# Depthwise convolution of a Conformer block: four channel tiles on TensorE from stacked shifted copies, four on VectorE

## The chip, the cores and the metric

The kernel runs on one core of a Trainium2 chip. The metric is device time in microseconds of one execution. Engines are named as in the profile: PE is TensorE's matmul side and PEld its weight load, DVE is VectorE, ACT is ScalarE, POOL is GpSimd, SP is SyncE, which here only issues DMA transfers.

## What is computed

A two-layer trunk on 512 tokens of width 1024: layer 0 is a causal Conformer convolution module and a top-2 mixture of 16 experts; layer 1 is sliding-window attention and the same kind of mixture. All is float32. The change concerns only the depthwise filter of this function (`CONV_WIDTH` is 31, `D_MODEL` 1024):

```python
def conformer_conv(x, w1, b1, dw, dwb, g, bn, w2, b2):
    h = x @ w1 + b1
    a, gate = jnp.split(h, 2, axis=-1)
    h = a * jax.nn.sigmoid(gate)
    h = lax.conv_general_dilated(
        h, dw[:, None, :].astype(h.dtype), window_strides=(1,),
        padding=[(CONV_WIDTH - 1, 0)], dimension_numbers=('NWC', 'WIO', 'NWC'),
        feature_group_count=D_MODEL) + dwb
    h = jax.nn.silu(layer_norm(h, g, bn))
    return h @ w2 + b2
```

Each channel is filtered by itself with 31 taps along the tokens.

## The kernel before

The kernel is written engine by engine. Each engine runs its own program in the order written, and the order between engines is held by semaphores: `wait_ge` and `then_inc`. There is no scheduler.

Channels lie on partitions in eight tiles of 128; tokens lie along the free dimension. `arena` is one buffer that holds `xT` (x transposed), `hpad` (the gated activations with 30 zero columns ahead), `cv` (the filtered result) and small pieces such as `odd` and `sgm`. `wring` is a ring of six slots of 2 MB for weights.

The first projection (L514) writes, for channel tile c, 8 matmuls of `a` and 8 of `gate` into two PSUM banks and signals `s_g1`. ScalarE takes the sigmoid of the gate (L1308, `s_sgm`). VectorE's `glu(c)` (L883) adds the bias, multiplies and writes `hpad` (`s_glu`). From tile 4 on, the projection waits for the `glu` of the tile four before it, to have its banks back.

Channel tiles 0 to 5 are filtered on VectorE: `taps(c)` has two opening instructions (L892, L894), 29 taps (L898) that alternate between two accumulators, and a closing sum (L901). Tiles 6 and 7 are filtered on TensorE: for each of 31 taps GpSimd has built a diagonal 128x128 matrix of that tap's weights (`diag(c)`, L1563, one instruction of 3968 columns for a tile), and 31 matmuls of 512 columns (L526) accumulate in one PSUM bank. ScalarE evicts the bank with the bias (L1316). Since the TensorE tiles are wanted early, VectorE's order is `glu` 0, `taps` 0, ..., `taps` 3, then `glu` 4, `glu` 6, `taps` 4, `glu` 5, `glu` 7, `taps` 5.

After that, `stage_a` to `stage_d` on TensorE transpose the result, normalise it, apply the second projection (L552), and route. The experts follow (L616 for gate and up, L626 for down). Each of their products has 64 rows of tokens; the stationary operand has 64 columns, and two products alternate between the lower and the upper 64 PSUM partitions:

```python
for j in range(4):
    for h in range(2):
        mm = pe.matmul(ps[h * CAP:(h + 1) * CAP, bank, :],
                       act[:, j % 2, (j // 2) * CAP:(j // 2 + 1) * CAP],
                       w[:, j, h * 512:(h + 1) * 512], start=(j == 0), stop=(j == 3))
```

In the trace one float32 matmul stands as two passes (two MATMUL records and two LDWEIGHTS records), so 62 matmuls of L526 are 124.

SyncE's queue after the convolution's weights: gate of expert 0 into slot 0 as soon as two channel tiles are projected, up after four, down after `s_pec` 1 and gate of expert 1 after `s_pec` 2 (`s_pec` counts tiles filtered on TensorE), then loads that wait for later stages. GpSimd scales x and adds the second projection's bias (L1557, L1558) before it builds the diagonals.

## Time and profile before

| | us |
|---|---|
| three runs | 1270.77, 1277.02, 1279.67 |
| median | 1277.02 |
| the profiled execution, its time | 1279.67 |
| the profiled execution, its span from first to last instruction | 1279.7 |
| PE busy | 1033.9 (81%) |
| DVE busy | 485.0 (38%) |
| POOL busy | 199.6 (16%) |
| ACT busy | 168.2 (13%) |

The busy shares are means over the whole program. The convolution stage lies in its first sixth; its limits are read from the chain of waits and from the timelines of that stretch, not from these shares. The span is the profiled execution's whole time, so nothing lies around it.

### The profile page before, as it was taken

What the parts mean: (1) busy time and instruction counts of PE and PEld (TensorE: products, weight loads), DVE (VectorE), ACT (ScalarE), POOL (GpSimd) and SP (SyncE); (2) the same over time, 40 slices, a digit from 0 to 9 for tenths busy, and PEclk for the clock granted to TensorE, in tenths of its full rate; (3) what the DMA queues carried; (4) which work ended last, traced back from release to release, by engine and by line L of the source; (5) the groups of instructions that cost most, each with busy time, mean ns of one, the idle gap of its engine ahead of it and who ended that gap; (6) DMA issues with size and microseconds to landing.
All of it is one profiled execution on the core that took longest, in us unless ns stands there. A gap on an engine that the chain in (4) does not pass through costs nothing.

```text
span 1279.7 us, 15066 instructions
## 1 busy us (share of the span) xinstructions
PE 1033.9 (81%) x5458; PEld 552.4 (43%) x5459; DVE 485.0 (38%) x1003; ACT 168.2 (13%) x375; POOL 199.6 (16%) x257
## 2 busy tenths in 40 slices
PE   5999597993799889999488899968369777999950
PEld 3444244542455445455134444534245444555520
DVE  1799991446111011101285456564510000110117
ACT  0000002212000000000103332432200000000010
POOL 2243601112200100100241002021210010000013
PEclk8999798986799999999788799878679898999985
DMA  9930011206399999988790001300738999897863
GB/s 296 401 116 0 0 66 66 82 34 223 116 345 380 356 401 338 381 290 361 253 323 39 1 1 66 148 1 34 246 104 314 382 391 390 296 378 294 359 217 112
DMA packets 59726, 275.04 MB, mean 215 GB/s; under 512 B 5469, under 2 KB 13833, under 8 KB 51352
## 3 DMA queue, kind: packets, MB, share of 16 engines
q1 hardware_dynamic: 40368, 226.50, 47.1%
q10 hardware_dynamic: 12952, 28.03, 5.9%
q0 software_dynamic: 6352, 19.77, 5.1%
q8 instruction: 36, 0.59, 0.2%
q14 instruction: 18, 0.15, 0.0%
HBM read 252.48 MB, written 21.80 MB: 214 GB/s over the span
## 4 chain that ended last, share of the span: by engine, by line
PE 60%; DMA 14%; DVE 12%; issue 9%; POOL 2%; ACT 2%; SPq 0%; DVEq 0%; ACTq 0%; POOLq 0%
PE ps L616 20%; PE ps L626 10%; PE ps L755 5%; DMA wring<-in_moe_w_gate_dram 5%; DMA wring<-in_moe_w_up_dram 5%; PE ps L552 5%; PE ps L526 4%; PE ps L774 4%; PE ps L609 3%; DVE arena L898 2%; DMA wring<-in_conv_w_dram 1%; PE ps L514 1%; POOL vareps L1590 1%; DVE bns L917 1%; PE ps L800 1%
## 5 line engine op out<-in xcount | busy, mean ns | idle before, releaser
L616 PE MATMUL ps<-wring,arena 128*64 128x256 f32 x2624 | 314.3, 396 | 40.1 <-DMA wring<-in_moe_w_gate_dram 18.3
L616 PEld LDWEIGHTS ps<-wring,arena 128*64 128x64 f32 x2624 | 195.2, 143 | 154.3 <-issue 54.6
L626 PE MATMUL ps<-wring,arena 128*64 128x512 f32 x688 | 157.0, 598 | 6.8 <-DVE arena L1108 5.7
L898 DVE SCALAR_TENSOR_TENSOR arena<-arena,dwT 128x512 f32<-128x512 f32 (+1 forms) x174 | 125.4, 799 | 0.0
L514 PE MATMUL ps<-arena,wring 128*128 128x512 f32 x256 | 113.1, 604 | 9.3 <-DMA wring<-in_conv_w_dram 9.3
L1095 DVE COPY arena<-ps 128x256 f32<-128x256 f32 x32 | 13.6, 425 | 239.6 <-PE ps L670 239.6
L755 PE MATMUL ps<-wring,arena 128*128 128x512 f32 x192 | 91.0, 631 | 6.3 <-DMA wring<-in_attn_wq_dram 2.9
L626 PEld LDWEIGHTS ps<-wring,arena 128*64 128x64 f32 x688 | 46.1, 136 | 85.3 <-issue 74.9
L514 PEld LDWEIGHTS ps<-arena,wring 128*128 128x128 f32 x256 | 49.4, 194 | 71.6 <-issue 71.6
L526 PE MATMUL ps<-arena,wring 128*128 128x512 f32 x124 | 55.9, 614 | 12.9 <-DVE arena L883 12.9
L1590 POOL TENSOR_SCALAR vareps<-mv 128x1 f32<-128x1 f32 x20 | 21.6, 1082 | 274.0 <-DVE mv L919 273.9
L1619 POOL COPY idx<-tokT 64x1 uint32 (+1 forms) x32 | 5.8, 181 | 374.2 <-PE ps L609 368.6
L1089 DVE TENSOR_TENSOR arena<-arena,ps 128x256 f32<-128x256 f32 x32 | 13.5, 422 | 132.1 <-PE ps L616 132.1
L774 PE MATMUL ps<-wring,arena 128*128 128x512 f32 x128 | 62.1, 641 | 0.0
L552 PE MATMUL ps<-wring,arena 128*128 128x512 f32 x128 | 60.5, 630 | 1.9 <-ACT arena L1328 1.3
L755 PEld LDWEIGHTS ps<-wring,arena 128*128 128x128 f32 x192 | 38.1, 204 | 52.9 <-issue 51.8
L609 PE MATMUL ps<-ident,arena 64*128 64x64 f32 x344 | 47.1, 279 | 10.5 <-DMA arena<-x_dram,idx 10.5
L609 PEld LDWEIGHTS ps<-ident,arena 64*128 64x128 f32 x344 | 41.2, 199 | 31.5 <-issue 31.5
L1369 ACT ACTIVATE arena<-ps 128x512 f32<-128x512 f32 x32 | 19.1, 597 | 268.3 <-PE ps L626 268.3
L1609 POOL DMA_INDIRECT arena<-x_dram,idx x43 | 39.9, 928 | 32.4 <-POOL idx L1619 24.1
L526 PEld LDWEIGHTS ps<-arena,wring 128*128 128x128 f32 x124 | 24.3, 197 | 44.5 <-issue 30.8
L774 PEld LDWEIGHTS ps<-wring,arena 128*128 128x128 f32 x128 | 25.8, 208 | 31.6 <-issue 31.6
(209 smaller groups left out, 933.0 us busy)
## 6 DMA issues: line engine op xcount, KB each, us to landing
wring<-in_moe_w_up_dram SPq DMA_DIRECT2D x32, 2048.0 KB, 20.7
wring<-in_moe_w_down_dram SPq DMA_DIRECT2D x32, 2048.0 KB, 13.4
wring<-in_moe_w_gate_dram SPq DMA_DIRECT2D x30, 2048.0 KB
y_dram<-arena ACTq DMA_DIRECT2D x86, 128.0 KB, 8.1
wring<-in_conv_w_dram SPq DMA_DIRECT2D x8, 1024.0 KB, 11.7
wring<-in_conv_w_dram SPq DMA_DIRECT2D x2, 2048.0 KB, 17.8
y_dram<-arena ACTq DMA_DIRECT2D x1, 4096.0 KB, 27.7
x_dram<-x_sb ACTq DMA_DIRECT2D x8, 512.0 KB, 3.1
```

Source lines behind the costliest of these rows:

```text
L514: last = pe.matmul(ps[:, 2 * (c % 4) + h, :], w[:, k, h, (c % 2) * P:(c % 2) * P + P], xT[:, k, :], start=(k == 0), stop=(k == KD - 1))
L526: last = pe.matmul(ps[:, 2 * (c % 4) - 4, :], diag(c)[:, k, :], hpad[:, c, k:k + S], start=(k == 0), stop=(k == CW - 1))
L552: last = pe.matmul(ps[:, 4 + h, :], hc[t % 2][:, c, :], slot(4 + c // 4, 4)[:, c % 4, h * 512:(h + 1) * 512], start=(c == 0), stop=(c == K ...
L609: last = pe.transpose(ps[:, 0, j * CAP:(j + 1) * CAP], src[0:CAP, j::KD], ident[0:CAP, 0:CAP])
L616: mm = pe.matmul(ps[h * CAP:(h + 1) * CAP, bank, 0:256], act[:, k, :], w[:, k, h * 256:(h + 1) * 256], start=(k == 0), stop=(k == KD - 1))
L626: mm = pe.matmul(ps[h * CAP:(h + 1) * CAP, bank, :], act[:, j % 2, (j // 2) * CAP:(j // 2 + 1) * CAP], w[:, j, h * 512:(h + 1) * 512], sta ...
L755: last = pe.matmul(ps[:, bank, :], xTt[:, k, :], slot(at, KD)[:, k, :], start=(k == 0), stop=(k == KD - 1))
L774: last = pe.matmul(ps[:, bank, :], oT[t % 2][:, k, :], slot(3 + h, KD)[:, k, :], start=(k == 0), stop=(k == KD - 1))
L898: dve.scalar_tensor_tensor(out=acc, in0=hpad[:, one, k:k + S], scalar=dwT[:, one, k:k + 1], in1=acc, op0=ALU.mult, op1=ALU.add).then_inc(s ...
L1369: act.activation(ysb[b], ps[:, 4, :], ACT.Copy).then_inc(s_yc, 1)
L1590: own(pool.tensor_scalar(vareps[:, n:n + 1], mv[:, n, 1:2], EPS, None, ALU.add))
L1609: pool.indirect_dma_start(out=where[0:CAP, :], out_offset=None, in_=x_dram[:, :], in_offset=bass.IndirectOffsetOnAxis(ap=idx[:, idx_col:id ...
```

## The change

DVE_TILES goes from 6 to 4: VectorE filters channel tiles 0 to 3, TensorE 4 to 7. TensorE's way of filtering is another. The tile's 128 channels are four groups of 32. For group q, SyncE copies the group's 32 rows of `hpad` four times into a ring slot, each copy on 32 partitions of its own and shifted by s = 0..3 columns (`replicate`, 16 small transfers a tile). One matmul with 128 rows and 32 output columns then applies four taps at once to 32 channels; eight rounds with the moving operand advanced by four columns make 32 taps, the last being zero. The four groups of a round write the four 32-partition parts of one PSUM bank. The stationary operands of all rounds and groups (`wdw`, 128 partitions x 4096) are made by one GpSimd multiply of `wrep` (the weights, loaded by eight small transfers into `dw_a` and transposed on TensorE) and `fold` (which partition belongs to which of 32 channels, a VectorE reduction of the identity). `wdw` takes ring slot 0, the copies of tiles 4, 5, 6, 7 take slots 1, 2, 3, 1. VectorE's loop becomes straight code with each `glu` set between taps of an earlier tile. The first expert's loads wait for all four TensorE tiles.

```diff
-DVE_TILES = 6
+DVE_TILES = 4
+SHIFTS = 4
+GRP = P // SHIFTS
+ROUNDS = 8
+REPW = S + SHIFTS * (ROUNDS - 1)
...
+        dw_a = view(14080, SHIFTS, GRP)
+        wrep = view(14208, P)
+        fold = view(14336, GRP)
...
+        wdw = wring[:, 0, :].rearrange("p (r g n) -> p r g n", r=ROUNDS, g=SHIFTS * (KD - DVE_TILES))
+
+        def shifted(c):
+
+            slot_of = (1, 2, 3, 1)[c - DVE_TILES]
+            return wring[:, slot_of, 0:SHIFTS * REPW].rearrange("p (g n) -> p g n", g=SHIFTS)
...
-            sp.wait_ge(s_g1, 2)
+            def replicate(c):
+
+                sp.wait_ge(s_glu, c + 1)
+                for s in range(SHIFTS):
+                    for q in range(SHIFTS):
+                        sp.dma_start(shifted(c)[s * GRP:(s + 1) * GRP, q, :],
+                                     hpad[q * GRP:(q + 1) * GRP, c, s:s + REPW]).then_inc(s_rep[c - DVE_TILES], 16)
+
+            replicate(4)
+            replicate(5)
+            sp.wait_ge(s_g1, KD)
+            replicate(6)
+            sp.wait_ge(s_pec, 1)
+            replicate(7)
+            sp.wait_ge(s_pec, KD - DVE_TILES)
             gate(0, 0, 0)
-            sp.wait_ge(s_g1, 4)
             up(0, 0, 0)
-            sp.wait_ge(s_pec, 1)
             down(0, 0, 0)
-            sp.wait_ge(s_pec, 2)
             gate(0, 1, 1)
...
-                for c in range(KD):
+                for c in range(DVE_TILES):
                     pe.transpose(ps[:, 4, 32 * c:32 * c + CW], dw_r[:, c * P:(c + 1) * P], ident[0:CW, 0:CW])
+                pe.wait_ge(s_dwload, 16 * ROUNDS)
+                pe.transpose(ps[:, 5, P:2 * P], dw_a.rearrange("p s c -> p (s c)"), ident[:, :])
...
+            pe.wait_ge(s_wdw, 1)
             for c in range(DVE_TILES, KD):
-                pe.wait_ge(s_glu, glu_count(c))
-                pe.wait_ge(s_diag, c - DVE_TILES + 1)
-                for k in range(CW):
-                    last = pe.matmul(ps[:, 2 * (c % 4) - 4, :], diag(c)[:, k, :], hpad[:, c, k:k + S],
-                                     start=(k == 0), stop=(k == CW - 1))
+                pe.wait_ge(s_glu, c + 1)
+                pe.wait_ge(s_rep[c - DVE_TILES], 16 * SHIFTS * SHIFTS)
+                for r in range(ROUNDS):
+                    for q in range(SHIFTS):
+                        last = pe.matmul(ps[q * GRP:(q + 1) * GRP, 2 * (c % 4), :],
+                                         wdw[:, r, SHIFTS * (c - DVE_TILES) + q, :],
+                                         shifted(c)[:, q, SHIFTS * r:SHIFTS * r + S],
+                                         start=(r == 0), stop=(r == ROUNDS - 1))
                 last.then_inc(s_pec, 1)
...
+            dve.tensor_copy(wrep, ps[:, 5, P:2 * P])
+            dve.wait_ge(s_pool0, 2)
+            dve.tensor_reduce(fold, ident[:, :].rearrange("p (s j) -> p j s", s=SHIFTS), AX.X, ALU.add)
...
-            with dve.Fori(0, 2) as i:
-                for b in range(2):
-                    glu(2 * i + b, b)
-                    taps(2 * i + b, 2 * i + (b + 1))
-            glu(4, 0)
-            glu(6, 0)
-            taps(4, glu_count(4))
-            glu(5, 1)
-            glu(7, 1)
-            taps(5, glu_count(5))
+            glu(0)
+            taps(0, {18: 1})
+            taps(1, {4: 2, 22: 3})
+            taps(2, {7: 4, 26: 5})
+            taps(3, {10: 6, 28: 7})
...
+            act.wait_ge(s_dwzero, 1)
+            groups = SHIFTS * (KD - DVE_TILES)
+            for r in range(ROUNDS):
+                n = min(SHIFTS, CW - SHIFTS * r)
+                act.dma_start(dw_a[groups * r:groups * (r + 1), 0:n, :],
+                              conv_dw[0, SHIFTS * r:SHIFTS * r + n, P * DVE_TILES:].rearrange("s (g c) -> g s c", c=GRP)
+                              ).then_inc(s_dwload, 16)
...
             pool.wait_ge(s_prC, 1)
-            for c in range(DVE_TILES, KD):
-                pool.wait_ge(s_g1, c if c < KD - 1 else KD)
-                pool.affine_select(out=diag(c), in_=dwT[:, c, 0:CW].unsqueeze(2).to_broadcast([P, CW, P]),
-                                   compare_op=ALU.is_equal, fill=0.0, base=0, pattern=[[0, CW], [-1, P]],
-                                   channel_multiplier=1).then_inc(s_diag, 1)
+            pool.wait_ge(s_g1, 2)
+            pool.tensor_tensor(wdw.rearrange("p r g n -> p (r g) n"), wrep.unsqueeze(2).to_broadcast([P, P, GRP]),
+                               fold.unsqueeze(1).to_broadcast([P, P, GRP]), ALU.mult).then_inc(s_wdw, 1)
```

In `taps(1, {4: 2, 22: 3})` the table says that `glu(2)` stands before tap 4 and `glu(3)` before tap 22 of channel tile 1.

TensorE, from the last tile of the projection to the first transpose of `stage_a`, before (L514 the projection, L526 the diagonal matmuls, L483 the transposes):

```order
L514 MATMUL ps<-arena,wring 128x512 [waits s_glu,s_w1_3]
L514 MATMUL ps<-arena,wring 128x512 x15
L526 MATMUL ps<-arena,wring 128x512 [waits s_diag,s_glu]
L526 MATMUL ps<-arena,wring 128x512 x30
L526 MATMUL ps<-arena,wring 128x512 [waits s_diag,s_glu]
L526 MATMUL ps<-arena,wring 128x512 x30
L483 MATMUL ps<-ident,arena 128x128 [waits s_tap,s_pecv]
```

and with the change (L534 the projection, L548 the new matmuls, L501 the transposes):

```order
L534 MATMUL ps<-arena,wring 128x512 [waits s_glu,s_w1_3]
L534 MATMUL ps<-arena,wring 128x512 x15
L548 MATMUL ps<-wring 32x512 [waits s_rep0,s_glu,s_wdw]
L548 MATMUL ps<-wring 32x512 x31
L548 MATMUL ps<-wring 32x512 [waits s_rep1,s_glu]
L548 MATMUL ps<-wring 32x512 x31
L548 MATMUL ps<-wring 32x512 [waits s_rep2,s_glu]
L548 MATMUL ps<-wring 32x512 x31
L548 MATMUL ps<-wring 32x512 [waits s_rep3,s_glu]
L548 MATMUL ps<-wring 32x512 x31
L501 MATMUL ps<-ident,arena 128x128 [waits s_tap,s_pecv]
```

Two runs of 31 matmuls with 128 output columns have become four runs of 32 with 32 output columns, and each run waits for its own copies (`s_rep0` to `s_rep3`).

SyncE, from the second projection's weights on, before:

```order
L403 DMA wring<-in_conv_w_dram 128x4x1024 x2
L406 DMA wring<-in_moe_w_gate_dram 128x4096 [waits s_g1]
L409 DMA wring<-in_moe_w_up_dram 128x4096 [waits s_g1]
L412 DMA wring<-in_moe_w_down_dram 128x4x1024 [waits s_pec]
L406 DMA wring<-in_moe_w_gate_dram 128x4096 [waits s_pec]
```

and with the change (`wring<-arena` are the copies):

```order
L447 DMA wring<-arena 32x540 [waits s_glu]
L447 DMA wring<-arena 32x540 x15
L447 DMA wring<-arena 32x540 [waits s_glu]
L447 DMA wring<-arena 32x540 x15
L447 DMA wring<-arena 32x540 [waits s_glu,s_g1]
L447 DMA wring<-arena 32x540 x15
L447 DMA wring<-arena 32x540 [waits s_glu,s_pec]
L447 DMA wring<-arena 32x540 x15
L413 DMA wring<-in_moe_w_gate_dram 128x4096 [waits s_pec]
L416 DMA wring<-in_moe_w_up_dram 128x4096
L419 DMA wring<-in_moe_w_down_dram 128x4x1024
L413 DMA wring<-in_moe_w_gate_dram 128x4096
```

Four runs of 16 transfers stand ahead of the first expert's loads, and these now wait for the last of the filtered tiles only.

VectorE, its last two channel tiles before (L883 `glu`, L892 and L894 openers, L898 taps, L901 sum):

```order
L883 SCALAR_TENSOR_TENSOR arena<-ps,prmT,arena 128x512 x2
L892 TENSOR_SCALAR arena<-arena,dwT,prmT 128x512
L894 TENSOR_SCALAR arena<-arena,dwT 128x512
L898 SCALAR_TENSOR_TENSOR arena<-arena,dwT 128x512 x29
L901 TENSOR_TENSOR arena<-arena 128x512
L883 SCALAR_TENSOR_TENSOR arena<-ps,prmT,arena 128x512 x2
L892 TENSOR_SCALAR arena<-arena,dwT,prmT 128x512
L894 TENSOR_SCALAR arena<-arena,dwT 128x512
L898 SCALAR_TENSOR_TENSOR arena<-arena,dwT 128x512 x29
L901 TENSOR_TENSOR arena<-arena 128x512
```

and the last channel tile with the change (L909 `glu`, L917 and L921 openers, L927 taps, L930 sum), after the sum of the tile before:

```order
L930 TENSOR_TENSOR arena<-arena 128x512
L917 TENSOR_SCALAR arena<-arena,dwT,prmT 128x512
L921 TENSOR_SCALAR arena<-arena,dwT 128x512
L927 SCALAR_TENSOR_TENSOR arena<-arena,dwT 128x512 x8
L909 SCALAR_TENSOR_TENSOR arena<-ps,prmT,arena 128x512
L927 SCALAR_TENSOR_TENSOR arena<-arena,dwT 128x512 x18
L909 SCALAR_TENSOR_TENSOR arena<-ps,prmT,arena 128x512
L927 SCALAR_TENSOR_TENSOR arena<-arena,dwT 128x512 x3
L930 TENSOR_TENSOR arena<-arena 128x512
```

The two `glu` of the TensorE tiles stand between taps now, `glu(7)` three taps before the end.

## Rows read from the trace of the kernel before

**Rows 1.** Chain of waits: shares by engine, then pieces (start us, us, what)
```profile
PE 60%; DMA 14%; DVE 12%; issue 9%; POOL 2%; ACT 2%; SPq 0%; DVEq 0%; ACTq 0%; POOLq 0%
...
328.00 9.64 PE ps L616 x64
```

**Rows 2.** Timeline of TensorE (start us, us, engine line operation count [idle before <-releaser])
```profile
37.99 96.46 PE L514 MATMUL ps<-arena,wring 128*128 128x512 f32 x224
...
147.37 55.89 PE L526 MATMUL ps<-arena,wring 128*128 128x512 f32 x124 [12.91 <-DVE arena L883]
...
204.03 1.09 PE L483 MATMUL ps<-ident,arena 128*128 128x128 f32 x8 [0.78 <-ACT arena L1316]
```

**Rows 3.** Timeline of VectorE: the weight copy, then pieces of channel tiles 0 to 5
```profile
38.29 0.41 DVE L873 COPY dwT<-ps 128x248 f32<-128x248 f32 x1
...
40.97 0.55 DVE L892 TENSOR_SCALAR arena<-arena,dwT,prmT  x1 [0.41 <-DVE arena L883]
...
93.41 0.69 DVE L901 TENSOR_TENSOR arena<-arena 128x512 f32 x1
...
115.58 4.09 DVE L901 TENSOR_TENSOR arena<-arena 128x512 f32 x1
...
146.56 0.75 DVE L883 SCALAR_TENSOR_TENSOR arena<-ps,prmT,arena 128x512 f32<-128x512 f32 x1 [0.89 <-ACT arena L1308]
...
148.11 20.28 DVE L898 SCALAR_TENSOR_TENSOR arena<-arena,dwT 128x512 f32<-128x512 f32 x29
...
171.33 0.54 DVE L892 TENSOR_SCALAR arena<-arena,dwT,prmT 128x512 f32<-128x512 f32 x1
...
172.18 19.30 DVE L898 SCALAR_TENSOR_TENSOR arena<-arena,dwT 128x512 f32<-128x512 f32 x29
...
191.51 0.69 DVE L901 TENSOR_TENSOR arena<-arena 128x512 f32<-128x512 f32 x1
```

**Rows 4.** GpSimd beside VectorE's taps: timeline; taps' durations, two windows; GpSimd groups
```profile
76.66 2.92 POOL L1558 TENSOR_TENSOR x_sb<-x_sb,rows 128x1024 f32<-128x1024 f32 x1
...
107.07 12.06 POOL L1563 TENSOR_SCALAR_AFFINE_SELECT wring<-dwT 128x3968 f32<-128x3968 f32 x1 [27.49 <-PE ps L514]
...
L898 DVE SCALAR_TENSOR_TENSOR arena<-arena,dwT x23: 737/740/2831, 53.8 to 81.4; - x12, 128x512 f32<-128x512 f32 x11
...
L898 DVE SCALAR_TENSOR_TENSOR arena<-arena,dwT x13: 743/744/746, 106.9 to 114.8; - x7, 128x512 f32<-128x512 f32 x6
...
L1684 POOL TENSOR_TENSOR x_sb<-x_sb,rows 128x1024 f32<-128x1024 f32 x4 | 9.6, 2394 | 0.3
```

**Rows 5.** L626's passes in narrow windows (busy, x open passes); chain in the experts
```profile
348.09:348.20 0.11, 0.10 (x2) 1.00 1.10 298
...
348.57:348.62 0.05, 0.05 (x4) 1.00 0.82 164
...
343.54 3.60 PE ps L616 x32
...
348.17 3.58 PE ps L626 x16
```

**Rows 6.** Timelines of DMA issues: ScalarE's queue, SyncE's queue
```profile
1.45 0.57 ACTq L1277 DMA_DIRECT2D prm<-in_conv_dwb_dram  x1
...
2.06 0.28 ACTq L1278 DMA_DIRECT2D prm<-in_conv_ln_g_dram  x1
...
0.85 1.83 SPq L397 DMA_DIRECT2D x_sb<-in_x_dram  x4
...
52.02 0.34 SPq L406 DMA_DIRECT2D wring<-in_moe_w_gate_dram  x1
```

**Rows 7.** DMA issues in 0 to 340 us (KB each, median us to landing)
```profile
x_sb<-in_x_dram SPq DMA_DIRECT2D x4, 512.0 KB, 5.2
...
tok_r<-tok_dram POOLq DMA_DIRECT2D x1, 32.0 KB, 2.5
```

**Rows 8.** Busy time by stretch: the experts of layer 0
```profile
328.00:613.00 285.00, 263.98 (x1935) 148.46 (x1936) 32.30 (x63) 20.41 (x42) 21.89 (x39) 0.97 0.90 338
```

More of the change, by code:

```diff
@@ L168, in view @@
             return v
-        PADW = S + CW - 1
+        PADW = REPW + SHIFTS
         xT = view(0, KD, S)
@@ L235, in trunk @@
         s_tap = sem("s_tap")
-        s_diag = sem("s_diag")
+        s_dwzero = sem("s_dwzero")
+        s_dwload = sem("s_dwload")
+        s_wdw = sem("s_wdw")
+        s_rep = [sem(f"s_rep{i}") for i in range(KD - DVE_TILES)]
         s_pec = sem("s_pec")
@@ L367, in taken @@
             eng.wait_ge(bank_read[bank - 5], n)
-        glu_order = [0, 1, 2, 3, 4, 6, 5, 7]
-        def glu_count(c):
-            return glu_order.index(c) + 1
-        def diag(c):
-            return wring[:, 2 + c - DVE_TILES, 0:CW * P].rearrange("p (k n) -> p k n", k=CW)
+        wdw = wring[:, 0, :].rearrange("p (r g n) -> p r g n", r=ROUNDS, g=SHIFTS * (KD - DVE_TILES))
+        def shifted(c):
+            slot_of = (1, 2, 3, 1)[c - DVE_TILES]
+            return wring[:, slot_of, 0:SHIFTS * REPW].rearrange("p (g n) -> p g n", g=SHIFTS)
         def slot(i, *dims):
@@ L861, in own @@
                 dve.wait_ge(s_dc, done[0])
+            dve.memset(dw_a.rearrange("p s c -> p (s c)"), 0.0).then_inc(s_dwzero, 1)
             for t in range(T):
@@ L874, in _, with glu @@
                             ).then_inc(s_prC, 1)
-            dve.wait_ge(s_pool0, 2)
             dve.wait_ge(s_prC, 1)
-            def glu(c, parity):
-                one = bass.ds(c, 1)
-                bank = 2 * c if not isinstance(c, int) else 2 * (c % 4)
+            def glu(c):
                 dve.wait_ge(s_g1, c + 1)
                 dve.wait_ge(s_sgm, c + 1)
-                dve.scalar_tensor_tensor(out=hpad[:, one, CW - 1:PADW], in0=ps[:, bass.ds(bank, 1), :],
-                                         scalar=prmT[:, bass.ds(c + PB1, 1)], in1=sgm[parity],
+                dve.scalar_tensor_tensor(out=hpad[:, c, CW - 1:CW - 1 + S], in0=ps[:, 2 * (c % 4), :],
+                                         scalar=prmT[:, PB1 + c:PB1 + c + 1], in1=sgm[c % 2],
@@ L885, in glu @@
                                          op0=ALU.add, op1=ALU.mult).then_inc(s_glu, 1)
             def taps(c, glus):
-                one = bass.ds(c, 1)
-                even = cv[:, one, :]
-                dve.wait_ge(s_glu, glus)
-                dve.tensor_scalar(even, hpad[:, one, 0:S], dwT[:, one, 0:1],
-                                  prmT[:, bass.ds(c + PDWB, 1)], ALU.mult, ALU.add).then_inc(s_tap, 1)
-                dve.tensor_scalar(odd, hpad[:, one, 1:1 + S], dwT[:, one, 1:2], None, ALU.mult).then_inc(s_tap, 1)
+                even = cv[:, c, :]
@@ L895, in taps @@
+                dve.wait_ge(s_glu, c + 1)
+                dve.tensor_scalar(even, hpad[:, c, 0:S], dwT[:, c, 0:1], prmT[:, PDWB + c:PDWB + c + 1],
+                                  ALU.mult, ALU.add).then_inc(s_tap, 1)
+                if c:
+                    dve.wait_ge(s_tap, c * (CW + 1))
+                dve.tensor_scalar(odd, hpad[:, c, 1:1 + S], dwT[:, c, 1:2], None, ALU.mult).then_inc(s_tap, 1)
                 for k in range(2, CW):
+                    if k in glus:
+                        glu(glus[k])
@@ L896, in taps @@
                     acc = (even, odd)[k % 2]
                     dve.wait_ge(s_tap, c * (CW + 1) + (k - 1))
-                    dve.scalar_tensor_tensor(out=acc, in0=hpad[:, one, k:k + S], scalar=dwT[:, one, k:k + 1],
+                    dve.scalar_tensor_tensor(out=acc, in0=hpad[:, c, k:k + S], scalar=dwT[:, c, k:k + 1],
                                              in1=acc, op0=ALU.mult, op1=ALU.add).then_inc(s_tap, 1)
@@ L1306, in _ @@
                 if c >= 2:
-                    act.wait_ge(s_glu, glu_count(c - 2))
+                    act.wait_ge(s_glu, c - 1)
                 act.activation(sgm[c % 2], ps[:, 1 + 2 * (c % 4), :], ACT.Sigmoid,
@@ L1524, in _ @@
             pool.memset(cv[:, KD - 1, :], 0.0)
+            pool.memset(hpad[:, :, CW - 1 + S:PADW], 0.0)
             pool.memset(hpad[:, :, 0:CW - 1], 0.0).then_inc(s_pool0, 1)
```

5 lines of the change are left out of this document (3 added, 2 removed).

## The prediction

> **What bounds the kernel now.** I read the chain of waits first. TensorE is 60% of it, and its list in order of time holds one block that belongs to this change: the 124 passes of L526 from 147.37 to 203.26, the depthwise filters of channel tiles 6 and 7 [rows 1, 2]. The reader is to see what stands on both sides of that block. Ahead of it TensorE idles 12.91 us, because it has finished the first projection at 134.45 but VectorE reaches `glu(6)` only at 146.56 [rows 3]; behind it ScalarE evicts and `stage_a` begins at 204.03 [rows 2]. So the end of the stage is VectorE's first four tiles, then 56 us of TensorE. VectorE's own last tile ends at 192.20 [rows 3]: 11 us of cover, no more. Everything after 203.3 (the rest of layer 0, attention, experts) is fed by that one point. Nothing that the change touches comes later, except loads of the first expert's weights. So the gain or loss is the shift of the point 203.26.
>
> **Work that goes.** TensorE loses 62 full matmuls, 55.89 us. VectorE loses two channel tiles. A tile in the clear costs it 20.87 us, 171.33 to 192.20: two openers, 29 taps at 0.665 (19.30/29), one sum [rows 3]. The pause around each `glu`, 0.4 us before and after, goes too, since a `glu` now sits between taps of an earlier tile and costs 0.67. GpSimd loses two diagonal builds, one of them 12.06 us; it did not slow the taps (13 of them at 0.743 to 0.746 us in its window), but the closing sum of a tile waited it out: 4.09 instead of 0.69 us [rows 3, 4].
>
> **TensorE's new work.** Each of four tiles takes 8 rounds of 4 matmuls, with 32 output columns each; a matmul stays two passes in the trace. A 512-column pass alone costs 96.46/224 = 0.4306 us [rows 2]. What four passes on four column groups cost together is the question on which all hangs. The nearest rows are the experts' products, where two groups of 64 columns alternate. In L626 two passes stand in the record at once from the start: 2 in the window 348.09 to 348.20, 4 from 348.57 as the next pair enters before the first drains; 16 passes take 3.58 us, 0.224 each, and 32 passes of half the width take 3.60 us [rows 5]. So two groups run wholly beside each other. Moreover the first pair starts together: if a pass waited behind all passes ahead of it, the second pass of the first matmul would have to go before the other group's first, and the first pass would stand alone. I read that as a queue for each group, in which case four groups overlap as well: 0.4306/4 = 0.1077 us a pass, 64 passes = 6.9 us a tile, 27.6 us for four. The bounds: as two groups do, 0.2153 a pass and 13.8 us a tile; with no overlap, 27.6 us a tile. I take 6.9, because the rows show full overlap at two and no sign of a limit. The instruction rate is no obstacle: the 0.1125 us a pass of the half-width products [rows 5] is about what four groups need.
>
> The Trainium skill, "TensorE: Matmul & The Clock Gate", section "Part 3: Packing small matmuls — row/col tiling", gives 2.38 times for three column tiles and 3.07 times for four row tiles, short of the ideal. No row here has more than two groups, and at two the trace shows no such loss. By that rule the sum would hold 8.6 to 9 us a tile instead of 6.9; it is the second rival below.
>
> **When each tile can start.** TensorE needs `wdw`, the projection's end at 134.45, and four shifted copies a tile. Nothing in the projection waits longer than now, so 134.45 stays. Tile 4 then runs to 141.3 and tile 5 to 148.2, if their copies have landed; they are asked for after `glu(4)` and `glu(5)`, in VectorE's third tile, over 10 us earlier. Copies 6 wait for the projection's last pass, 134.45. Copies 7 wait for tile 4's matmuls (their slot) and for `glu(7)`, which stands three taps before VectorE's end.
>
> One `replicate` is 16 issues on SyncE. Their nearest rows are 0.28 to 0.57 us on ScalarE's queue, small tables, and 0.34 and 0.46 on SyncE's for big tiles [rows 6]. I take 0.40, 6.4 us for 16; bounds 4.5 and 9.1. From the last issue to landing I take 2.4, near the 2.5 of the token table, with 5.2 of the x tiles as upper end and 2.0 as lower [rows 7]. A copy set is thus there 8.8 us (6.5 to 14.3) after its release. Tile 6: 134.45 + 8.8 = 143.3, before TensorE wants it at 148.2. Tile 7 depends on VectorE.
>
> **VectorE's new length.** It starts later by the weight table's copy and the reduction to `fold`: estimate 0.4 us from the 0.41 of the copy of 248 columns [rows 3]. So first `glu` at 40.2, first tap 41.4. Then four clear tiles 83.5, seven `glu` 4.7, the present loss to GpSimd's work on x, and a new one. The present loss: the first two tiles run from 40.97 to 94.1, 53.1 us, against 2 x 20.87 and an estimate of 1.1 for the second `glu` with its pauses: 10.3 us. Nearly all of it is one pattern: the tap that starts beside GpSimd's L1558, a tensor_tensor of 1024 columns, lasts 2.83 us and ends with it [rows 4]. The new `wdw` is such a tensor_tensor with 4096 columns. Uncontended, 1024 take 2.39 [rows 4], so 9.6 us, directly behind L1558, 79.6 to 89.2, ahead of anything needing it by 45 us. But it holds VectorE for about 9.1 of them. Bounds: nothing, if it behaves as the diagonal build, whose 12.06 us left taps alone; 12.1 if it takes the diagonal's rate with full blocking. I take 9.1, for L1558 is the same operation. GpSimd's rope steps, which stretched one tile from 19.30 to 20.28, add 1.0 [rows 3]. Sum: 41.4 + 83.5 + 4.7 + 10.3 + 9.1 + 1.0 = 150.0. `glu(7)` ends 2.7 us earlier, at 147.3.
>
> The Trainium skill, "SBUF — State Buffer", section "Who interferes with whom", says that a VectorE instruction with two SBUF inputs contends with any GpSimd instruction that reads SBUF, and that the second to issue blocks fully. The rows agree for L1558 and disagree for the diagonal build. It would leave the sum at 9.1, and turns my doubt to the other bound.
>
> **The sum.** Copies 7 land at 147.3 + 8.8 = 156.1; TensorE, done with tile 6 at 155.0, waits a microsecond, and ends at 156.1 + 6.9 + 0.1 = 163.1. The stage behind it is unchanged: 163.1 against 203.26 is 40.2 us. VectorE, done at 150.0, covers nothing and waits for nobody. Two small items: the eight short loads of `dw_a` share the queues with the first projection weights (estimate 0 to 1 us: 64 KB beside the megabytes that keep the queues full until 20.6), and the transpose of `dw_a` stands in for four small ones, 0. Loads of gate, up, down and the second gate now all start at 163: 8 MB at the 338 GB/s of the expert phase [rows 8] are 25 us, done at 188, long before the experts, now at 328.0 [rows 1], then at about 288. They are covered by the 100 us of stages between.
>
> Against the profiled execution, 1279.7 us span and time, this gives 1239.5. That execution is the slowest of three; from the median, 1277.0, it gives 1237 us.
>
> **Rivals.**
> The overlap is short of four: a pass costs 0.1345 us (a quarter of the way from 0.1077 to 0.2153), 8.6 us a tile, because four streams of moving data are read at once where the rows have two. For: nothing in these rows measures it. Against: no loss from one to two. TensorE 134.45 + 34.4 = 168.9: 34 us saved, 1243.
> Only two groups overlap at any time: 13.8 us a tile, 134.45 + 55.2 = 189.6, 14 us saved, 1263. For: passes in program order come two by two for one group, so a queue in strict order would give exactly this at four groups, and the same picture of pairs but for the first. Against: that first pair.
> VectorE becomes the bound: if `wdw` with its broadcast operands takes twice its time, `glu(7)` comes 9.6 later, copies 7 at 165.7, end at 172.7: 30 us saved, 1247.
> The other side: column groups of 32 do not run beside each other. Then 128 matmuls cost 0.861 each, 110.2 us, and the end is 244.7: 41 us lost, 1318. It decides at (203.26 - 134.45)/128 = 0.54 us a matmul, an overlap of 1.6; above that price the kernel is slower. For: no row has 32-column groups. Against: the 64-column rows have an overlap of 2.
>
> **How the numbers follow.** Full overlap 0.60; short of four 0.13; VectorE's bound 0.07; two by two 0.11; no overlap 0.09. Forecast 1237. The three runs before spread from 1270.8 to 1279.7, so a change under 1%, 13 us, can hardly be told from none. The range goes from 1228 (the fastest of the runs before less 41, and a little) to 1262, which takes in the first three cases and half of two by two. Faster by over 1% has those 0.80 and half of two by two less a margin: 0.83; within 1% the rest of it and small unseen losses, 0.08; slower 0.09.
>
> **What the profile after would show.** The passes on `wring` with 32 columns: 256 of them in 28 to 29 us, begun at 134 to 135, with full clock; a gap of about a microsecond before the last 64. One tap of 9 to 10 us from 79 to 90. SyncE's 16 issues a set at 0.4 us. The first expert about 40 us sooner, and a phase behind it of the same length. The forecast is wrong if the four groups' passes start 0.2 us apart or more, or if copies arrive later than 14 us after their release, which costs TensorE the difference four times.

## The result, and the profile after

| | median | lowest to highest | ratio to before |
|---|---|---|---|
| before, 4 runs | 1275.8 us | 1270.77 to 1279.67 | |
| the changed kernel, 4 runs | 1240.53 us | 1236.38 to 1244.44 | 0.9712 (0.968 to 0.9744) |

The numbers in brackets behind a ratio are its 95% interval, here and below. The kernel is 35.3 us faster, where 40 were forecast. The profiled execution after has a span of 1238.1 us and a time of 1239.92. Its time stands 1.8 us above its span, and in every later run it is 1.6 to 1.8; the equal numbers in the table of before are therefore probably of two executions. Traces are compared here by spans: 1279.7 against 1238.1.

The page of the changed kernel, its chain of waits by engine and by line:

```profile
PE 67%; DMA 13%; DVE 9%; issue 4%; POOL 2%; ACT 2%; SPq 2%; ACTq 0%; POOLq 0%; DVEq 0%
```

Against [rows 1] TensorE's share is larger and a new member has come in, SPq, SyncE issuing. Where it sits shows in the timelines of the changed kernel, TensorE and then SyncE's queue:

```profile
133.67 20.81 PE L548 MATMUL ps<-wring 128*32 128x512 f32 x192
157.19 8.77 PE L548 MATMUL ps<-wring 128*32 128x512 f32 x64 [2.71 <-DMA wring<-arena]
166.76 1.09 PE L501 MATMUL ps<-ident,arena 128*128 128x128 f32 x8 [0.80 <-ACT arena L1346]
```

```profile
108.00 47.64 SPq L447 DMA_DIRECT2D wring<-arena  x64
166.01 0.35 SPq L413 DMA_DIRECT2D wring<-in_moe_w_gate_dram  x1
```

L548 is the new filter. It starts right behind the projection at 133.67, where L526 waited until 147.37 [rows 2]. The first 192 passes, three tiles, take 20.81 us without a gap: 0.1084 us a pass. A 512-column pass alone costs 0.4306 [rows 2], so four run at once: 0.4306/0.1084 = 3.97. Then TensorE waits 2.71 us for copies, and the last tile takes 8.77 us instead of 6.9. The filters end at 165.96, against 203.26: 37.3 us sooner.

That all four groups are fed at the same time shows in narrow windows of the changed kernel (window, length, TensorE busy with x passes open):

```profile
133.67:134.10 0.43, 0.43 (x5) 0.16 (x8) 0.43 (x2) 0.32 (x1) 0.00 (x0) 1.00 0.00 0
134.10:134.50 0.40, 0.40 (x8) 0.13 (x4) 0.40 (x1) 0.37 (x1) 0.00 (x0) 1.00 0.00 0
```

One open pass at the start is the projection's last, four are L548's first; they start 6.7 ns apart. The next four come 0.45 us later, and from then on four every 0.43 us. In [rows 5] the same picture had two.

Who held the last tile? The chain of waits of the changed kernel names it:

```profile
133.78 0.51 SPq L447
134.32 0.59 SPq L447
...
144.76 0.54 SPq L447
...
154.42 0.59 SPq L447
155.05 2.00 DMA wring<-arena
157.06 0.14 issue
157.19 8.80 PE ps L548 x64
```

It holds the issues of the 16 copies of tile 6 from 133.8 and of tile 7 from 144.8, nearly all of them 0.59 us with 0.04 between. Two were longer (1.46 and 1.13), so that the last of the 32 begins 21.3 us after the first, at 155.05. It lands 2.00 us after that; the median of all 64 copies is 2.0 as well, so the transfers themselves don't pile up. SyncE's queue is the bound from 133.8 to 155.

VectorE and GpSimd in the changed kernel, beside the one long tap:

```profile
71.51 23.84 DVE L927 SCALAR_TENSOR_TENSOR arena<-arena,dwT 128x512 f32<-128x512 f32 x18
...
143.91 0.74 DVE L909 SCALAR_TENSOR_TENSOR arena<-ps,prmT,arena 128x512 f32<-128x512 f32 x1
144.57 2.06 DVE L927 SCALAR_TENSOR_TENSOR arena<-arena,dwT 128x512 f32<-128x512 f32 x3
146.67 0.69 DVE L930 TENSOR_TENSOR arena<-arena 128x512 f32<-128x512 f32 x1
```

```profile
76.40 2.92 POOL L1589 TENSOR_TENSOR x_sb<-x_sb,rows 128x1024 f32<-128x1024 f32 x1
79.28 7.54 POOL L1593 TENSOR_TENSOR wring<-arena 128x4096 f32<-128x4096 f32 x1
```

And the taps of that group of 18, by duration (ns, min/median/max):

```profile
L927 DVE SCALAR_TENSOR_TENSOR arena<-arena,dwT x18: 739/773/7571, 71.5 to 94.4; 128x512 f32<-128x512 f32 x18
```

L1593 is the making of `wdw`, 7.54 us, and one tap beside it lasts 7.57. `glu(7)` is L909 at 143.91. It ends at 144.65, just when SyncE is done with tile 6's copies; VectorE is done at 147.36.

Behind the filters, TensorE's first block of the second projection, before and after, and its first products of the first expert after:

```profile
215.08 10.57 PE L552 MATMUL ps<-wring,arena 128*128 128x512 f32 x24 [1.29 <-ACT arena L1328]
```

```profile
177.81 12.27 PE L576 MATMUL ps<-wring,arena 128*128 128x512 f32 x24 [1.29 <-ACT arena L1358]
...
292.94 9.27 PE L640 MATMUL ps<-wring,arena 128*64 128x256 f32 x64 [0.94 <-DVE arena L1105]
```

From the filters' end to the first expert's products it is 127.0 us, against 124.7 from 203.26 to 328.00 before [rows 1, 2]. So the first expert begins 35.1 us sooner, not 37.3. Of the 2.2 us between, 1.7 are this first block: 12.27 us instead of 10.57. The granted clock was 0.50 in its first 2.2 us, and 1.00 in the first 2.9 us of the same block before:

```profile
177.81:180.00 2.19, 2.19 (x3) 1.16 (x4) 1.16 (x3) 0.00 (x0) 0.79 (x2) 0.50 1.00 413
```

The block took 10.57 us in both profiles of the kernel before and in two of the changed and edited ones, and 12.1 to 12.8 us in the rest, so the clock there differs from run to run. Whether the change makes the lower clock likelier is open. The expert phase, from 292.94 to 588.08, is 295.1 us long, against 293.6 before. From the filters' end to the end of the span it is 1076.4 us before and 1072.1 after. Those 4.3 us don't come from the stages just behind the filters: behind the experts it is 650.0 us against 658.1. They are the spread of an execution: the same stretch takes 1070.2 us in a second profile of the kernel before, and 1065 to 1078 us in the other runs, which differ only ahead of it.

### The profile page after: what moved, and what is told of

It reads as the page before. It is cut to its first block, busy times and chain, and to the rows that moved or that the text cites. A ratio compares the mean times of both kernels' runs of the same rounds, so it can differ in the third digit from the quotient of the medians.

```text
span 1238.1 us, 15187 instructions
## 1 busy us (share of the span) xinstructions
PE 1001.9 (81%) x5587; PEld 534.3 (43%) x5588; DVE 444.1 (36%) x942; ACT 169.6 (14%) x377; POOL 186.2 (15%) x257
## 4 chain that ended last, share of the span: by engine, by line
PE 67%; DMA 13%; DVE 9%; issue 4%; POOL 2%; ACT 2%; SPq 2%; ACTq 0%; POOLq 0%; DVEq 0%
PE ps L640 22%; PE ps L650 11%; PE ps L534 9%; PE ps L779 5%; DMA wring<-in_moe_w_gate_dram 5%; PE ps L576 5%; PE ps L798 4%; DMA wring<-in_moe_w_up_dram 4%; PE ps L633 3%; SPq L447 2%; DMA wring<-in_conv_w_dram 1%; POOL vareps L1619 1%; DVE bns L940 1%; PE ps L824 1%; PE ps L850 1%
## 5 line engine op out<-in xcount | busy, mean ns | idle before, releaser
L640 PE MATMUL ps<-wring,arena 128*64 128x256 f32 x2624 | 310.0, 392 | 42.4 <-DMA wring<-in_moe_w_gate_dram 16.9
L534 PE MATMUL ps<-arena,wring 128*128 128x512 f32 x256 | 112.1, 600 | 9.5 <-DMA wring<-in_conv_w_dram 9.5
L927 DVE SCALAR_TENSOR_TENSOR arena<-arena,dwT 128x512 f32<-128x512 f32 x116 | 93.7, 879 | 0.0
L534 PEld LDWEIGHTS ps<-arena,wring 128*128 128x128 f32 x256 | 49.1, 193 | 71.0 <-issue 71.0
L779 PEld LDWEIGHTS ps<-wring,arena 128*128 128x128 f32 x192 | 38.5, 206 | 53.5 <-issue 52.4
L1638 POOL DMA_INDIRECT arena<-x_dram,idx x43 | 39.8, 926 | 32.4 <-POOL idx L1648 24.1
L576 PEld LDWEIGHTS ps<-wring,arena 128*128 128x128 f32 x128 | 25.9, 208 | 33.2 <-issue 31.6
L798 PEld LDWEIGHTS ps<-wring,arena 128*128 128x128 f32 x128 | 24.8, 200 | 30.1 <-issue 30.0
L1689 POOL DMA_INDIRECT arena<-y_dram,rowi x16 | 17.3, 1084 | 123.0 <-DMA y_dram<-arena 119.0
## 6 DMA issues: line engine op xcount, KB each, us to landing
wring<-in_conv_w_dram SPq DMA_DIRECT2D x2, 2048.0 KB, 17.6
y_dram<-arena ACTq DMA_DIRECT2D x1, 4096.0 KB, 22.3
```

What stands on the lines that cost most here:

```text
L534: last = pe.matmul(ps[:, 2 * (c % 4) + h, :], w[:, k, h, (c % 2) * P:(c % 2) * P + P], xT[:, k, :], start=(k == 0), stop=(k == KD - 1))
L576: last = pe.matmul(ps[:, 4 + h, :], hc[t % 2][:, c, :], slot(4 + c // 4, 4)[:, c % 4, h * 512:(h + 1) * 512], start=(c == 0), stop=(c == K ...
L640: mm = pe.matmul(ps[h * CAP:(h + 1) * CAP, bank, 0:256], act[:, k, :], w[:, k, h * 256:(h + 1) * 256], start=(k == 0), stop=(k == KD - 1))
L779: last = pe.matmul(ps[:, bank, :], xTt[:, k, :], slot(at, KD)[:, k, :], start=(k == 0), stop=(k == KD - 1))
L798: last = pe.matmul(ps[:, bank, :], oT[t % 2][:, k, :], slot(3 + h, KD)[:, k, :], start=(k == 0), stop=(k == KD - 1))
L927: dve.scalar_tensor_tensor(out=acc, in0=hpad[:, c, k:k + S], scalar=dwT[:, c, k:k + 1], in1=acc, op0=ALU.mult, op1=ALU.add).then_inc(s_tap, 1)
```

## The experiments

Four kernels ran on one chip with 11 runs of before (median 1273.7), six timed runs each; edits are against the changed kernel.

**The change again**, no edit.

> The changed kernel once more, as the measure for the other three of this call. Ratio to the kernel before 0.971 as first measured, 1237 to 1243 us.

Measured: 1241.67 us, ratio 0.9768 (0.9733 to 0.9804). TensorE's timeline repeats:

```profile
134.10 20.81 PE L548 MATMUL ps<-wring 128*32 128x512 f32 x192
157.70 8.77 PE L548 MATMUL ps<-wring 128*32 128x512 f32 x64 [2.80 <-DMA wring<-arena]
```

The late and slow last tile belongs to the kernel. The gain, 32.0 us, is clear of noise, though the interval reaches past 0.98, so a gain of 2% isn't certain on this chip.

**One queue, nothing else in the way.** Tile 7's copies go to the space of the transposed x, free since the projection; SyncE no longer waits for tile 4, and `glu(7)` stands 12 taps earlier.

```
-            slot_of = (1, 2, 3, 1)[c - DVE_TILES]
+            if c == 7:
+                return view(0, SHIFTS, REPW)
...
-            sp.wait_ge(s_pec, 1)
             replicate(7)
...
-            taps(3, {10: 6, 28: 7})
+            taps(3, {10: 6, 16: 7})
```

> The copies of tile 7 go to space that the projection's input leaves free, so they wait neither for tile 4's matmuls nor, with glu(7) moved from tap 28 to tap 16, for VectorE; all 32 issues stay on SyncE's queue. Theory (issue rate): 32 issues at 0.63 us from 133.8 end at 154.5, nearly as in the change (155.4), so under 1.5 us is won. Rival (the slot wait or glu(7) holds the last tile, as the prediction had it): the end of the filters falls to 161 to 162, 4 us won.

Measured: 1239.51 us, ratio 0.9741 (0.9705 to 0.9777), not to be told from the change, as the theory of the issue rate had it. SyncE's queue, then TensorE:

```profile
108.10 36.38 SPq L449 DMA_DIRECT2D wring<-arena  x48
144.52 11.26 SPq L449 DMA_DIRECT2D arena<-arena  x16
```

```profile
157.33 8.77 PE L549 MATMUL ps<-arena,wring 128*32 128x512 f32 x64 [2.65 <-DMA arena<-arena]
```

`glu(7)` ended at 136.8 here, nearly 8 us sooner than after the change, and the slot was free. Tile 7's copies were still issued from 144.52 to 155.78, and TensorE's wait is the same. So neither VectorE nor the slot held them: it was the rate of issue.

**Two queues.** Half of the copies of tiles 6 and 7 are issued by ScalarE (`replicate_half`, eight copies), all else as in the change.

```
-                for s in range(SHIFTS):
+                for s in range(SHIFTS if c < 6 else 2):
...
+            act.wait_ge(s_g1, KD)
+            replicate_half(6)
             for c in range(DVE_TILES, KD):
                 act.wait_ge(s_pec, c - DVE_TILES + 1)
+                if c == 5:
+                    replicate_half(7)
```

> Of the 16 copies of tile 6 and of tile 7, eight each go out on ScalarE's queue instead of SyncE's. Theory (SyncE's issue rate holds the last tile: 16 issues at 0.63 us, 10 us a set, of which set 7 starts behind set 6): set 6 is out by 139, set 7 starts at 144.7 when glu(7) is done and is out by 150, landed at 152; TensorE has tile 6 done at 154.3, does not wait 2.7 us, keeps its full clock, and the last 64 passes take 6.9 instead of 8.8 us. End of the filters 161.2 instead of 166.0: 4 to 5 us less than the change. Rival (the two queues share one path that issues, or the transfers themselves are slow): issues take 1.2 us each and nothing is won.

Measured: 1237.82 us, ratio 0.9708 (0.9671 to 0.9746). TensorE, and ScalarE's queue:

```profile
155.03 7.07 PE L548 MATMUL ps<-wring 128*32 128x512 f32 x64 [1.02 <-DMA wring<-arena]
```

```profile
133.39 6.73 ACTq L1348 DMA_DIRECT2D wring<-arena  x8
147.21 6.26 ACTq L1348 DMA_DIRECT2D wring<-arena  x8
```

Two queues beside each other help, but not by half: 8 issues take 6.7 and 6.3 us on ScalarE's queue, 0.84 and 0.78 each in the mean, where SyncE's alone needs 0.63. Whether ScalarE's queue is slower by itself was not tried. Its half of tile 7 begins at 147.21 and not at 144.2, when `glu(7)` is done, because ScalarE waits for tile 5's filters (`s_pec` 2) first in this edit; the wait that is left comes from this. It fell from 2.80 to 1.02 us, and the last tile from 8.77 to 7.07. From the projection's end to the filters' it is 28.9 us (133.20 to 162.1) instead of 32.4. The times agree (1237.82 against 1241.67), but their intervals overlap; the stage shows the gain, not the time.

**Both edits together**, and ScalarE issues tile 7's half ahead of its evictions.

> Both of the above: two queues, the free space for tile 7, glu(7) at tap 16. Theory: set 7 is out by 145, far ahead of need; the end of the filters is 161, TensorE works from 20.7 to 161 without a pause: 4 to 5 us less than the change, the same as with two queues alone, since TensorE's own work is then the bound. Rival (VectorE's glu(7) is what two queues alone leave as the bound): this one is 2 us or more below two queues alone.

Measured: 1235.0 us, ratio 0.9681 (0.9643 to 0.972). No wait is left:

```profile
133.93 20.81 PE L549 MATMUL ps<-wring 128*32 128x512 f32 x192
154.55 7.05 PE L549 MATMUL ps<-arena,wring 128*32 128x512 f32 x64
```

From the projection's end to the filters' it is 27.7 us, four tiles in the clear. That is 1.2 us less than with two queues alone, where the theory had no difference; the 2.8 us between the medians are not clear of noise. This is the fastest version that ran; its interval and that of the change on the same chip (0.9733 to 0.9804) don't meet. The stage is now TensorE's projection and filters back to back.

Four kernels had one run each on another chip, beside one run of before (1278.08 us), so that a difference of a few us in their times says nothing; their traces are what counts. They test how TensorE feeds its column groups, and the covers that the sum rests on.

**Groups one after the other.** The eight rounds of group 0, then those of group 1, and so on.

```
-                for r in range(ROUNDS):
-                    for q in range(SHIFTS):
+                for q in range(SHIFTS):
+                    for r in range(ROUNDS):
```

> The same 128 matmuls and operands as in the change, but each column group does its eight rounds before the next group begins, so that neighbours in the queue are of one group. Theory (passes overlap only when neighbouring matmuls are of different groups): 0.43 us a pass, 27.5 us a tile, the filters end at about 244 instead of 166, the run is some 78 us longer than the change, 1318 us. Rival (each group has a deep queue of its own and TensorE runs ahead over eight matmuls, 16 passes): the overlap stays, 28 us for all, 1240 us.

Measured: 1299.88 us. TensorE, then narrow windows of it:

```profile
135.19 84.75 PE L548 MATMUL ps<-wring 128*32 128x512 f32 x256
```

```profile
135.19:138.60 3.41, 3.41 (x9) 0.90 (x9) 3.41 (x6) 0.69 (x1) 0.00 (x0) 1.00 0.33 79
138.60:140.30 1.70, 1.70 (x5) 0.44 (x4) 1.70 (x4) 0.00 (x0) 0.00 (x0) 1.00 0.40 95
140.30:143.80 3.50, 3.50 (x13) 0.97 (x12) 3.50 (x6) 0.00 (x0) 0.00 (x0) 1.00 0.48 114
```

The expectation of no overlap was missed, and so was the rival of full overlap. In the first two windows one pass is open at a time (8 in 3.41 us and 4 in 1.70, at 0.43 each, and one at the edge); in the third 12, so for half of it two groups run. A group has 16 passes, 6.9 us alone. The next group's first pass starts 5.18 us after its own, when four of the 16 are left. (The records don't name the group; that two groups run is read from passes that start closer together than the 0.43 us one group needs.) Sixteen groups then take 15 x 5.18 + 6.89 = 84.6 us; 84.75 were measured.

**Groups two by two:** all rounds of groups 0 and 1, then of 2 and 3.

```
-                for r in range(ROUNDS):
-                    for q in range(SHIFTS):
+                for r, q in [(r, q) for h in (0, 2) for r in range(ROUNDS) for q in (h, h + 1)]:
```

> Groups 0 and 1 alternate through their eight rounds, then groups 2 and 3. Theory: two passes at once, 0.215 us a pass, 13.8 us a tile, 55 us for four tiles; the filters end at about 189 instead of 166, 1262 us. This is the price of the forecast's second rival. Rival (reach over eight matmuls): as the change, 1240 us.

Measured: 1251.68 us.

```profile
133.09 43.37 PE L547 MATMUL ps<-wring 128*32 128x512 f32 x256
```

Missed in the same direction, and by the same rule: eight pairs take 7 x 5.18 + 6.88 = 43.1 us. Here eight passes are left when the next pair begins, four in each group; four ahead for all groups together would have given about 49 us. So each column group takes work ahead, four passes (two matmuls) of it, and holds up those behind it in the program only when it has these. The Trainium skill, "TensorE: Matmul & The Clock Gate", section "Part 3: Packing small matmuls — row/col tiling", says that matmuls start and end strictly in program order. These two traces don't agree: group 0's last passes start after group 1's first.

**The glus where they were:** `glu(c)` ahead of `taps(c)`, those of tiles 4 to 7 after `taps(3)`.

```
-            glu(0)
-            taps(0, {18: 1})
...
+            for c in range(DVE_TILES):
+                glu(c)
+                taps(c, {})
+            for c in range(DVE_TILES, KD):
+                glu(c)
```

> VectorE's order is as in the kernel before: glu(c) right before taps(c), and glu 4 to 7 after taps(3). Theory: glu(4) comes at about 145, after which 64 issues of copies at 0.63 us go out in a row; set 4 lands at 157, set 7 at 187; TensorE idles from 134 and works one tile behind each set, at half clock in part; the filters end at 195 to 198, 30 us later than in the change, 1270 us: the change would be worth next to nothing without the placed glus. Rival (the copies are not what TensorE waits for): 145 + 28 = 173, 1247 us.

Measured: 1275.66 us, span 1274.0. The filters' end is the expected one, the time 6 us above the expected 1270.

```profile
158.63 9.08 PE L548 MATMUL ps<-wring 128*32 128x512 f32 x64 [17.64 <-DMA wring<-arena]
169.67 7.07 PE L548 MATMUL ps<-wring 128*32 128x512 f32 x64 [1.96 <-DMA wring<-arena]
179.79 8.75 PE L548 MATMUL ps<-wring 128*32 128x512 f32 x64 [3.04 <-DMA wring<-arena]
190.72 7.07 PE L548 MATMUL ps<-wring 128*32 128x512 f32 x64 [2.19 <-DMA wring<-arena]
```

Tiles come at the pace of SyncE, 10.1 to 11 us a set, not of TensorE. With the glus late nearly the whole gain is gone: the filters end at 197.8. TensorE is idle from 141.0 and not from 134, since the projection's last tile itself waits 4.41 us for `glu(3)` in this order. In the changed kernel the early glus let 32 of the 64 issues, from 108.00 on, go out while the projection runs.

**`wdw` by another GpSimd operation:** four selects of 32 partitions in place of the multiply.

```
-            pool.tensor_tensor(wdw.rearrange("p r g n -> p (r g) n"), wrep.unsqueeze(2).to_broadcast([P, P, GRP]),
-                               fold.unsqueeze(1).to_broadcast([P, P, GRP]), ALU.mult).then_inc(s_wdw, 1)
+            pool.wait_ge(s_xa, T)
+            for s in range(SHIFTS):
+                part = slice(s * GRP, (s + 1) * GRP)
+                own(pool.affine_select(out=wflat[part], in_=wrep[part].unsqueeze(2).to_broadcast([GRP, P, GRP]),
+                                       compare_op=ALU.is_equal, fill=0.0, base=0, pattern=[[0, P], [-1, GRP]],
+                                       channel_multiplier=1))
+            pool.sem_inc(s_wdw, 1)
```

> The stationary operands are made by four GpSimd selects over 32 partitions each, 4096 columns, instead of one tensor_tensor. Theory (a GpSimd tensor_tensor holds VectorE's taps for its whole length and a select does not, but holds the tile's closing sum and openers): the tap of 7.57 us is gone; four selects of about 12 us stand from 79 to 127, and the one or two closing sums that meet them wait up to 12 us each. The end of the filters does not move (SyncE's issues bound it), or by VectorE's delay if two sums meet selects: 1238 to 1250 us. Rival (any GpSimd instruction that reads the same memory blocks a tap with two inputs there): taps of 12 us, VectorE's end at 185 and 1280 us.

Measured: 1258.26 us. GpSimd, then the durations of VectorE's taps:

```profile
79.97 19.61 POOL L1597 TENSOR_SCALAR_AFFINE_SELECT wring<-arena 32x4096 f32<-32x4096 f32 x4 [0.16 <-PE ps L534]
```

```profile
L927 DVE SCALAR_TENSOR_TENSOR arena<-arena,dwT x18: 735/772/5022, 76.2 to 107.1; 128x512 f32<-128x512 f32 x18
```

The expectation fell. The selects were to take 12 us each. The diagonal select of 12.06 us did not hold taps [rows 4]; these selects, 4.9 us each, hold one tap each, for 5.01 to 5.02. VectorE ends 12.8 us later than after the change, at 160.1: 8.0 of it in the 18 taps beside the selects (31.87 us against 23.84), 4.7 ahead of them, where more taps stood beside GpSimd's work on x. Those 4.7 are not the edit's: with groups one after the other, which leaves VectorE and GpSimd alone, the same 18 taps begin at 76.62, against 76.21 here and 71.51 after the change. This is the rival in which VectorE is the bound, come true; the chain of waits now goes through `glu(7)`:

```profile
155.98 0.76 DVE arena L927
156.74 0.68 DVE arena L909
157.47 0.51 SPq L447
...
167.85 2.00 DMA wring<-arena
169.86 0.14 issue
169.99 8.77 PE ps L548 x64
```

From `glu(7)` to the last tile it is 12.6 us. The Trainium skill, "SBUF — State Buffer", section "Who interferes with whom", has a VectorE instruction with two SBUF inputs contend with any GpSimd instruction that reads SBUF. These selects and the multiply agree; the diagonal select of before doesn't. What sets the two selects apart was not tried: the width (32 or 128 partitions), or the buffer read (`arena`, where the taps' own operands lie, or `dwT`).

On a third chip, with 13 runs of before (median 1277.79):

**Six tiles on VectorE**, two on TensorE in the new way (`DVE_TILES = 6`, slots 3 and 1, half of `wdw`, taps of tiles 4 and 5 in the clear).

> Only TensorE's way of filtering is changed; the division stays as in the kernel before, channel tiles 0 to 5 on VectorE, 6 and 7 on TensorE by column groups. wdw is half as wide (2048 columns, about 3.8 us of GpSimd). Theory (the parts each give about half): TensorE is done with both tiles by 165, VectorE by 147.4 + 2 x 20.9 less 3.8, 185 to 186; stage_a begins at 186 instead of 204 (before) and 167 (change): 17 to 18 us less than the kernel before, 1257. Rival (the whole gain comes from the division of work, since VectorE's six tiles end at 192 before and bound the stage): 1265 or more.

Measured: 1261.58 us, ratio 0.9873 (0.9857 to 0.989): the time is some 4 us above the theory, the stage's end as the theory had it. VectorE, and TensorE:

```profile
184.99 0.69 DVE L927 TENSOR_TENSOR arena<-arena 128x512 f32<-128x512 f32 x1
```

```profile
145.26 9.43 PE L545 MATMUL ps<-wring 128*32 128x512 f32 x64 [11.74 <-DMA wring<-arena]
156.43 7.07 PE L545 MATMUL ps<-wring 128*32 128x512 f32 x64 [1.75 <-DMA wring<-arena]
185.82 1.94 PE L498 MATMUL ps<-ident,arena 128*128 128x128 f32 x8 [22.32 <-DVE arena L927]
```

TensorE is done at 163.5 and waits 22.3 us for VectorE. The stage ends at 185.7, 17.6 us before 203.26, and 16.2 us show in the time. So of the 37.3 us about 18 come from the new filtering together with the early glus, and about 20 from the two tiles that this lets VectorE hand over. No run separates the early glus from the new filtering with six tiles on VectorE. An estimate from the rows: 62 diagonal matmuls at 0.861 us, straight behind the projection's end at 134.45, would end at 187.9, 15 us before 203.26, and VectorE's six tiles, done at 185.7 here, would not hold it up. So most of those 18 us would probably have come from the early glus alone. What four column groups at once give is above all that TensorE can take four tiles: with diagonal matmuls four would take 107 us.

**The kernel before again**, no edit.

> The kernel before against itself. It shows how far a second profile's time after the filters differs from the first's, 1076.4 us from 203.26 to the end. Theory (what follows the filters varies by some us from run to run, whatever the kernel): ratio 1.00, filters end within 1 us of 203.3, the rest 1068 to 1078 us. Rival (the change gives 3 to 4 us back after the filters, by its later expert loads): the rest is 1070 or less in this second profile too, while the changed kernel's two profiles have 1072 and 1073.

Measured: 1275.39 us (10 runs), ratio 0.9976 (0.9955 to 0.9997). The filters end at 202.7 instead of 203.26, and the rest takes 1070.2 us instead of 1076.4, within the expected bounds. The rival isn't borne out: the change's two profiles, 1072.1 and 1073.0, lie between these two. An apparent difference of 0.2% between equal kernels, with an interval that leaves out 1, says how far a ratio can be trusted here.

## Why the prediction was right, and which term was off

**Right: the bound and the cover.** The sum was made at one point, the end of the filters, and what lies behind it moved with it but for 2.2 us: the first expert's products begin at 292.94 instead of 328.00, 35.1 us sooner and not 40. The projection's end was to stay at 134.45; it came at 133.67, and at 133.1 to 135.2 in the other runs that don't hold it up, so that this 0.8 us is spread. The eight small loads of `dw_a` took 3.81 us of ScalarE's queue, and the first projection pass is 0.1 us later. The loads that now wait for all four tiles cost nothing: ahead of the first expert's products TensorE waits 0.94 us for VectorE, as before, and not for a load.

**Right: four groups overlap.** 0.1077 us a pass was forecast, 0.1084 measured, from rows that had two groups. The Trainium skill's 2.38 times for three column tiles (the page and section cited in the prediction) doesn't hold for these matmuls: the trace shows 3.97 times for four, so the rival with a pass of 0.1345 us is out, and the rival without overlap too. Of the two-by-two rival the reading was half right: passes do go to the groups in program order, but each group takes four ahead, which with rounds outside and groups inside is more than is needed.

**Mis-sized: the issue of a copy.** "I take 0.40, 6.4 us for 16; bounds 4.5 and 9.1" is the term that was mis-sized: it was 0.63 us each, and with one or two longer issues in some sets 10.0 to 11.3 us for 16, above the upper bound. The landing, taken as 2.4 us, was 2.0. The nearest rows were issues of tables from HBM; a copy within SBUF was not among them. With it the bound of the last tile changed hands: not `glu(7)` plus a set, 147.3 + 8.8 = 156.1, but two sets in a row from the projection's end, 133.8 + 21.3 + 2.0 = 157.1. That the two are only 1 us apart is luck: tile 7's set took 12.3 us from its first issue to the last landing instead of 8.8, but it could begin at 144.76 instead of 147.3. The run with one queue and an early `glu(7)` shows that this is the cause. That late copies cost TensorE the difference four times, as the prediction says at its end, would not hold in this order: the sets of tiles 4 and 5 were out by 131.3, while the projection ran, and only tile 7's was late.

**Not foreseen: the clock behind the wait.** The forecast had a wait of 1 us, then 6.9 us. It was 2.71 us, and the tile behind it took 8.77. Windows of the changed kernel (granted clock third from the end):

```profile
157.20:160.30 3.10, 3.10 (x16) 0.96 (x20) 0.00 (x0) 0.00 (x0) 0.00 (x0) 0.53 0.00 0
160.30:165.96 5.66, 5.66 (x52) 1.85 (x44) 0.00 (x0) 0.00 (x0) 0.00 (x0) 0.96 0.00 0
```

In the first 3.1 us the granted clock is 0.53, close to the 1.2 GHz level, after full clock (1.00) up to the wait and in it. At half clock half of that time's work is missing. The tile takes 7.05 us where it ran without a wait, since its last pass stands in the record for 0.59 us and not 0.43, and so 1.7 of its 8.77 us are the clock's. The terms together: the last tile starts 1.1 us later (157.2 against 156.1), the clock costs 1.7, and the last pass 0.05 beyond the 0.1 of the forecast, which is the 2.9 us between 40.2 and 37.3.

**VectorE's length: errors that cost nothing.** `glu(7)` ended at 144.65, 2.7 us sooner than forecast. The first opening instruction came at 40.03, not 41.4. `wdw` took 7.54 us, not 9.6, and cost VectorE 6.9 and not 9.1. The rest, mostly waits beside GpSimd's work on x, came to about 0.9 us more than forecast, the closing sum of tile 0 (2.82 us) among them. The 2.7 us gained nothing, since SyncE was the bound.

**From span to median.** 1277.0 - 40.2 was forecast. With what was measured, 1275.8 - 37.3 = 1238.5, against 1240.5; by the first expert's start it is 1275.8 - 35.1 = 1240.7. Either is inside the spread of the two kernels. The second comparison, with more runs, has 32.0 us.

## What to carry to other kernels

If a depthwise or other narrow product fills only 32 output columns, issue one matmul for each of the four column groups in turn: here four ran in the time of one (3.97 times). What then bounds is what feeds them; count each small DMA as issue time on its queue, and as soon as a set of issues takes longer than the matmuls that it feeds, start the sets earlier or split them over two queues. Before moving work between engines, find the one point that both must reach, and see who is late there after the move.

## What the runs showed of the hardware

- A column group of TensorE takes four 512-column passes ahead: with groups one after the other the next starts 5.18 us after the one before, with 16 passes in a group at 0.43 us, and pairs of groups follow each other at the same distance.
- A copy of 32 rows of 540 float32 within SBUF costs its queue 0.63 us to issue, 10.0 to 11.3 us for 16 of them, and 0.67 to 0.86 in the mean on ScalarE's queue while SyncE issues as well. It lands 2.0 us after its issue begins (median).
- TensorE's clock and the wait ahead of a tile: after waits of 1.02, 1.63, 1.75, 1.96 and 2.19 us a tile took 7.07 us; after 2.65, 2.71, 2.80, 3.04, 4.77, 6.20, 11.74 and 17.64 us it took 8.47 to 9.43. In the first 3 us of the tile the granted clock was 1.00 after the former and 0.50 to 0.61 after the latter. With the wait cut from 2.80 to 1.02 us the stage was 3.5 us shorter, not 1.8.
- GpSimd's multiply of 128x4096 with broadcast inputs took 7.54 us, less than four times the 2.39 of 1024 columns [rows 4], and held one tap of VectorE for all of it. One of 128x2048 took 4.08.
